# Starting TensorE's streamed operands and the split weights on 256-byte lines of SBUF

## The reference: what is computed

```python
# first block, two layers
h = h + rmsnorm(hgrn2_mixer(rmsnorm(h)))          # x @ w_in (1024 x 4096), gated recurrence, @ w_out
h = h + rmsnorm(conv_ffn(rmsnorm(h)))             # up (1024 x 2*2752), 3-tap conv, silu(gate)*value, down
h = h + rmsnorm(fox_mixer(rmsnorm(h), shared_kv)) # forget-gate attention, 16 heads
h = h + rmsnorm(conv_ffn(rmsnorm(h)))
# second block, two layers, each with shift, scale and gate from silu(c) @ ada_w + ada_b
x = x + gate * gdn_mixer(norm(x))                 # gated delta rule, 8 heads
x = x + gate * swiglu(norm(x))                    # gate and up (1024 x 2816 each), down
x = x + gate * mla_mixer(norm(x))                 # latent attention with rotary part
x = x + gate * swiglu(norm(x))
out = rmsnorm(x)
```

## The kernel before

| tensor | streamed width (columns) | row pitch in bytes | first row begins at (mod 256) | matmuls |
|---|---|---|---|---|
| `w_hi`, `w_lo` | stationary, 128 | 512 | 64 and 64 | all |
| `x_hi_a`, `x_lo_a` (HGRN in) | 272 | 1088 | 128 and 128 | 768 |
| `x_hi_b`, `x_lo_b` (HGRN out) | 272 | 1088 | 128 and 128 | 192 |
| `x_hi_up0`, `x_lo_up0` | 272 | 1088 | 128 and 128 | 1032 |
| `a_hi_up0`, `a_lo_up0` (down 0) | 272 | 1088 | 128 and 0 | 528 |
| `x_hi_c`, `x_lo_c` (Fox in) | 272 | 1088 | 128 and 128 | 600 |
| `fox_heads` (Fox out), from column 14 | 258 | 2176 | 184 | 192 |
| `x_hi_up1`, `x_lo_up1`, from column 14 | 258 | 1088 | 184 and 184 | 1032 |
| `a_hi_up1`, `a_lo_up1` (down 1) | 256 | 1024 | 128 and 128 | 528 |
| `x_hi_e`, `x_lo_e` (GDN in and out) | 256 | 1024 | 128 and 128 | 984 |
| `z_hi`, `z_lo` (gu0, gu1, MLA in) | 258 | 1032 | 128 and 192 | 2256 |
| `a_hi_gu`, `a_lo_gu` (dn0, dn1) | 256 | 1024 | 0 and 0 | 1055 |
| `xq_hi`, `xq_lo` | 256 | 1024 | 32 and 32 | 108 |
| `xkv_hi`, `xkv_lo` | 256 | 1024 | 0 and 0 | 48 streamed |
| `mla_o_hi`, `mla_o_lo` | 256 | 1024 | 0 and 0 | 192 |

## Time and profile before

### The profile page before, as it was taken

The page is one execution under the profiler, slowest core; times in us unless marked ns, Lnnn a source line. Parts: engine busy times, 40 slices in busy tenths (PEclk is TensorE's granted clock), DMA queues, the critical chain, the costliest instruction groups (busy, mean ns, idle before and its releaser), DMA issues. The chain is left out here.

```text
span 1529.3 us, 28962 instructions
## 1 busy us (share of the span) xinstructions
PE 1436.7 (94%) x11237; PEld 1380.1 (90%) x11237; DVE 1051.7 (69%) x1798; ACT 777.2 (51%) x1259; POOL 270.9 (18%) x360
## 2 busy tenths in 40 slices
PE   7998899999889998999979899989999999999997
PEld 7998789999888777999977799989999998899997
DVE  7773777877878726888777745357877657687653
ACT  6645554453476544454436555565343456544342
POOL 2001001220033400122001244002333100132210
PEclk9999989999999988999999999999999999999999
DMA  8533435559433203665953211136775635385451
GB/s 326 190 111 138 165 129 202 211 195 354 176 142 118 100 30 123 234 226 180 363 222 110 87 60 64 69 112 230 277 270 201 228 110 179 111 303 202 142 184 50
DMA packets 45700, 264.68 MB, mean 173 GB/s; under 512 B 8736, under 2 KB 10016, under 8 KB 20512
## 3 DMA queue, kind: packets, MB, share of 16 engines
q1 hardware_dynamic: 45600, 263.33, 47.6%
HBM read 262.26 MB, written 1.05 MB: 172 GB/s over the span
## 5 line engine op out<-in xcount | busy, mean ns | idle before, releaser
L257 DVE TENSOR_TENSOR w_lo<-raw,w_hi 128x2048 fp32r<-128x2048 f32 (+3 forms) x204 | 418.7, 2057 | 177.5 <-ACT w_hi L249 174.4
L249 ACT ACTIVATE w_hi<-raw 128x2048 fp32r<-128x2048 f32 (+3 forms) x221 | 380.1, 1725 | 83.0 <-PE bank L1233 43.4
L469 PE MATMUL bank<-z_hi,w_hi 128*128 128x258 f32 x704 | 199.9, 284 | 0.0
L471 PE MATMUL bank<-z_hi,w_lo 128*128 128x258 f32 x704 | 198.5, 282 | 0.0
L470 PE MATMUL bank<-z_lo,w_hi 128*128 128x258 f32 x704 | 198.2, 282 | 0.0
L470 PE MATMUL bank<-x_lo_up,w_hi 128*128 128x272 f32 (+1 forms) x656 | 188.1, 287 | 0.0
L469 PE MATMUL bank<-x_hi_up,w_hi 128*128 128x272 f32 (+1 forms) x656 | 187.2, 285 | 0.0
L471 PE MATMUL bank<-x_hi_up,w_lo 128*128 128x272 f32 (+1 forms) x656 | 186.6, 284 | 0.0
L470 PEld LDWEIGHTS bank<-z_lo,w_hi 128*128 128x128 f32 x704 | 133.4, 190 | 0.1
L471 PEld LDWEIGHTS bank<-z_hi,w_lo 128*128 128x128 f32 x704 | 133.0, 189 | 0.0
L469 PEld LDWEIGHTS bank<-z_hi,w_hi 128*128 128x128 f32 x704 | 132.8, 189 | 0.1
(11 more groups left out here) (516 smaller groups left out, 3924.2 us busy)
## 6 DMA issues: line engine op xcount, KB each, us to landing
raw<-w_gu SPq DMA_DIRECT2D x44, 1024.0 KB, 4.8
raw<-w_up SPq DMA_DIRECT2D x42, 1024.0 KB, 4.8
work<-w_ada SPq DMA_DIRECT2D x27, 1024.0 KB, 4.9
raw<-w_down SPq DMA_DIRECT2D x32, 704.0 KB, 5.4
raw<-w_dn SPq DMA_DIRECT2D x32, 704.0 KB, 4.1
mod_w_down<-w_ada SPq DMA_DIRECT2D x16, 1024.0 KB, 6.9
raw<-w_a_in SPq DMA_DIRECT2D x15, 1024.0 KB, 5.0
raw<-w_gdn_qkv SPq DMA_DIRECT2D x12, 1024.0 KB, 4.8
```

Source lines behind the costliest of these rows:

```text
L249: act.activation(w_hi[:, s, 0:blocks * P], raw[:, s, 0:blocks * P], ACT.Copy).then_inc(hi_split.sem, 1)
L257: dve.tensor_tensor(w_lo[:, s, 0:blocks * P], raw[:, s, 0:blocks * P], w_hi[:, s, 0:blocks * P].bitcast(F32), ALU.subtract).then_inc(lo_sp ...
L469: pe.matmul(o, w_hi[:, s, b], x_hi[:, xk, cols[0]:cols[1]], start=begin, stop=False)
L471: last = pe.matmul(o, w_lo[:, s, b], x_hi[:, xk, cols[0]:cols[1]], start=False, stop=end)
```

## The change

Every three-pass operand for which there is room gets rows whose pitch is rounded up to a multiple of 256 bytes and whose streamed part begins on one; `lead` shifts the row so that column 14 falls on the line where the stream begins there. `w_hi` and `w_lo` begin on a line. `x_c`, `a_up0` and `fox_heads` only get an aligned first row: the pitches of 1088 and 2176 bytes stay, so that their rows go on from one phase to the next, and `fox_heads` still streams from column 14. The remaining edits find the room: small tensors share `small_columns`, `gate_tok` shrinks from 128 to 104 columns (and the copy that fills it), and three scratch tensors of MLA move onto rooms that are free by then (`rope_other` onto `angles`, `angle_turns` and `probs_turned_mla` onto the constants' `levels`). No matmul, wait or DMA is added or removed.

```diff
+LINE = 256
-        def sbuf(c, name, shape, dt=F32):
-            return c.enter_context(nc.sbuf_tensor(name, shape, dt))
+        def sbuf(c, name, shape, dt=F32, align=32):
+            return c.enter_context(nc.sbuf_tensor(name, shape, dt, align_bytes=align))
+
+        def rows_on_lines(c, name, rows, width, lead=0):
+            pitch = -(-(lead + width) * 4 // LINE) * LINE // 4
+            return sbuf(c, name, [P, rows, pitch], F32R, LINE)[:, :, lead:lead + width]
-        w_hi = sbuf(ctx, "w_hi", [P, SLOTS, ITEM], F32R)
-        w_lo = sbuf(ctx, "w_lo", [P, SLOTS, ITEM], F32R)
+        w_hi = sbuf(ctx, "w_hi", [P, SLOTS, ITEM], F32R, LINE)
+        w_lo = sbuf(ctx, "w_lo", [P, SLOTS, ITEM], F32R, LINE)
+        small = sbuf(ctx, "small_columns", [P, 23])
-                x_hi, x_lo = sbuf(phase, "x_hi_a", [P, KD, T1], F32R), sbuf(phase, "x_lo_a", [P, KD, T1], F32R)
+                x_hi, x_lo = (rows_on_lines(phase, n, KD, T1) for n in ("x_hi_a", "x_lo_a"))
...
-                x_hi, x_lo = sbuf(phase, "x_hi_b", [P, KD, T1], F32R), sbuf(phase, "x_lo_b", [P, KD, T1], F32R)
+                x_hi, x_lo = (rows_on_lines(phase, n, KD, T1) for n in ("x_hi_b", "x_lo_b"))
...
-                a_hi = sbuf(phase, f"a_hi_{up}", [P, FF_TILES, width], F32R)
+                a_hi = sbuf(phase, f"a_hi_{up}", [P, FF_TILES, width], F32R, LINE)
-                    x_hi = sbuf(inner, f"x_hi_{up}", [P, KD, T1], F32R)
+                    x_hi = rows_on_lines(inner, f"x_hi_{up}", KD, T1, -cols[0] % (LINE // 4))
...
-                x_hi, x_lo = sbuf(inner, "x_hi_c", [P, KD, T1], F32R), sbuf(inner, "x_lo_c", [P, KD, T1], F32R)
+                x_hi, x_lo = (sbuf(inner, n, [P, KD, T1], F32R, LINE) for n in ("x_hi_c", "x_lo_c"))
...
-                        dve.tensor_copy(tok[:, :, :], bank[2][:, 0:2 * P].rearrange("p (x c) -> p x c",
-                                                                                   x=2)).then_inc(tok_made.sem, 1)
+                        turned_rows = bank[2][:, 0:2 * P].rearrange("p (x c) -> p x c", x=2)
+                        dve.tensor_copy(tok[:, :, :], turned_rows[:, :, 0:BR + H]).then_inc(tok_made.sem, 1)
...
-                xkv_hi, xkv_lo = (sbuf(scope, n, [P, 2, SEQ], F32R) for n in ("xkv_hi", "xkv_lo"))
-                other = sbuf(scope, "rope_other", [P, 2, SEQ])
+                xkv_hi, xkv_lo = (rows_on_lines(scope, n, 2, SEQ) for n in ("xkv_hi", "xkv_lo"))
+                other = angles
-                pt = sbuf(scope, "probs_turned_mla", [P, 2, 3 * C])
+                pt = con("levels", 0, 6 * C).rearrange("p (x c) -> p x c", x=2)
...
-            heads = sbuf(outer, "fox_heads", [P, KD, 2, T1], F32R)
+            heads = sbuf(outer, "fox_heads", [P, KD, 2, T1], F32R, LINE)
-            x_hi, x_lo = sbuf(scope, "x_hi_e", [P, KD, SEQ], F32R), sbuf(scope, "x_lo_e", [P, KD, SEQ], F32R)
+            x_hi, x_lo = (rows_on_lines(scope, n, KD, SEQ) for n in ("x_hi_e", "x_lo_e"))
-            z_hi, z_lo = (sbuf(scope, n, [P, KD, SEQ + 2], F32R) for n in ("z_hi", "z_lo"))
+            z_hi, z_lo = (rows_on_lines(scope, n, KD, SEQ + 2) for n in ("z_hi", "z_lo"))
-                a_hi, a_lo = (sbuf(phase, n, [P, FF_TILES, SEQ], F32R) for n in ("a_hi_gu0", "a_lo_gu0"))
+                a_hi, a_lo = (rows_on_lines(phase, n, FF_TILES, SEQ) for n in ("a_hi_gu0", "a_lo_gu0"))
...
-                    xq_hi, xq_lo = (sbuf(early, n, [P, 3, SEQ], F32R) for n in ("xq_hi", "xq_lo"))
-                o_hi, o_lo = (sbuf(phase, n, [P, KD, SEQ], F32R) for n in ("mla_o_hi", "mla_o_lo"))
+                    xq_hi, xq_lo = (rows_on_lines(early, n, 3, SEQ) for n in ("xq_hi", "xq_lo"))
+                o_hi, o_lo = (rows_on_lines(phase, n, KD, SEQ) for n in ("mla_o_hi", "mla_o_lo"))
```

More of the change, by code:

```diff
@@ L124, in fused_model @@
         std_room = sbuf(ctx, "std", [P, ROOT_COLS])
-        root_tok = sbuf(ctx, "root_tok", [P, ROOT_COLS // SQUARE])
         rstd, std = rstd_room[:, 0:T1], std_room[:, 0:T1]
@@ L129, in fused_model @@
         modf = mod[:, :, :, :].rearrange("p l s k -> p (l s k)")
-        mod_sum = sbuf(ctx, "mod_sum", [P, 2, 2])
         c_row = sbuf(ctx, "c_row", [P, D])
         raw = sbuf(ctx, "raw", [P, SLOTS, ITEM])
-        w_hi = sbuf(ctx, "w_hi", [P, SLOTS, ITEM], F32R)
-        w_lo = sbuf(ctx, "w_lo", [P, SLOTS, ITEM], F32R)
+        w_hi = sbuf(ctx, "w_hi", [P, SLOTS, ITEM], F32R, LINE)
+        w_lo = sbuf(ctx, "w_lo", [P, SLOTS, ITEM], F32R, LINE)
+        small = sbuf(ctx, "small_columns", [P, 23])
+        root_tok, mod_sum = small[:, 0:9], small[:, 9:13].rearrange("p (l t) -> p l t", l=2)
+        eps_col, conv_last, gate_coef, norm_eps = small[:, 13:14], small[:, 14:20], small[:, 20:22], small[:, 22:23]
         bank = [ctx.enter_context(nc.psum_tensor(f"bank{i}", [P, 512], F32)) for i in range(8)]
@@ L948, in passed @@
                     s_.passed(n_)
-        eps_col = sbuf(ctx, "eps_col", [P, 1])
-        conv_last = sbuf(ctx, "conv_last", [P, 6])
         params_in, consts_in, c_in = sig("params_in"), sig("consts_in"), sig("c_in")
@@ L1550, in ffn_layer @@
             with ExitStack() as phase:
-                a_hi = sbuf(phase, f"a_hi_{up}", [P, FF_TILES, width], F32R)
-                a_lo = sbuf(phase, f"a_lo_{up}", [P, FF_TILES, width], F32R)
+                a_hi = sbuf(phase, f"a_hi_{up}", [P, FF_TILES, width], F32R, LINE)
+                a_lo = sbuf(phase, f"a_lo_{up}", [P, FF_TILES, width], F32R, LINE)
                 with ExitStack() as inner:
-                    x_hi = sbuf(inner, f"x_hi_{up}", [P, KD, T1], F32R)
-                    x_lo = sbuf(inner, f"x_lo_{up}", [P, KD, T1], F32R)
+                    x_hi = rows_on_lines(inner, f"x_hi_{up}", KD, T1, -cols[0] % (LINE // 4))
+                    x_lo = rows_on_lines(inner, f"x_lo_{up}", KD, T1, -cols[0] % (LINE // 4))
                     entry = NormEntry(lambda k: h[:, k, cols[0]:cols[1]], KD, cols, gain, x_hi, x_lo, shift=shift,
@@ L2152, in __init__ @@
                 rows = sbuf(scope, "gate_rows", [P, SEQ])
-                tok = sbuf(scope, "gate_tok", [P, 2, P])
-                coef = sbuf(scope, "gate_coef", [P, 2])
+                G, B, R, BR = 0, 32, 64, 96
+                tok = sbuf(scope, "gate_tok", [P, 2, BR + H])
+                coef = gate_coef
                 one_col = con("reset_hgrn", 0, 47)
-                norm_eps = sbuf(scope, "head_norm_eps", [P, 1])
                 Lo = sbuf(scope, "coupling_level", [P, 2, 4, C])
@@ L2159, in __init__ @@
                 late_q = sbuf(scope, "late_queries", [P, H, C])
-                G, B, R, BR = 0, 32, 64, 96
                 grown, beta, lean = (tok[:, :, i:i + H] for i in (G, B, R))
@@ L3214, in fused_model @@
                     positions = sbuf(inner, "positions", [P, SEQ], mybir.dt.int32)
-                    turned = Angles(angles, sbuf(inner, "angle_turns", [P, 2, SEQ]), positions)
+                    turned = Angles(angles, con("levels", 0, 2 * SEQ).rearrange("p (x t) -> p x t", x=2), positions)
                     dn0 = streamed_down("dn0", a_hi, a_lo, res2, squares, mod_room(inner, "dn0"),
@@ L3227, in fused_model @@
                 run(gdn, gdn_out, gu0, dn0, mla_in, mla)
-            a_hi, a_lo = (sbuf(scope, n, [P, FF_TILES, SEQ], F32R) for n in ("a_hi_gu1", "a_lo_gu1"))
+            a_hi, a_lo = (rows_on_lines(scope, n, FF_TILES, SEQ) for n in ("a_hi_gu1", "a_lo_gu1"))
             res3 = Streamed("a", "mla_out", False, mod[:, 1, 2, :], squares, z_hi, z_lo, mod[:, 1, 4, :], mod[:, 1, 3, :])
```

## The result

The changed kernel takes 1540.64 us (median of 4 runs, 1537.96 to 1542.70), the kernel before 1530.55 us (4 runs, 1528.38 to 1531.77): a ratio of 1.0061, 95% interval 1.0045 to 1.0078. It is 0.6% slower. The forecast was 1504 us with the range 1490 to 1528, and 0.11 for slower: the sign is wrong.

What follows compares the result with a forecast made beforehand. The prediction took the count of matmuls times their start-to-start distance as the bound. Gains of 6.8 + 8.6 + 12.3 = 27.7 us, less 1.4 and 1.1, left 25.2 us: from 1529.6 to 1504.4 us, range 1490 to 1528.

Steps and rivals of the forecast that it cites:

- What bounds the kernel: Over most of the span, time is the number of matmuls times the start-to-start distance; TensorE's matmuls cover 94%.
- `w_hi`, `w_lo` from 64 to 0: Aligning the weight buffers, in all three-pass matmuls: taken as 0, with a possible gain of 16 us or a loss.
- excess per line: Each 256-byte line an operand row touches costs 1.7 ns per matmul; used to price gains at 258 and 272 columns.
- rival D: Weights and operand both at 0 collide; `a_gu` and `mla_o` fall back to 117.6 ns, costing 5.2 us: 1535 us; chance 0.09.
- Rival A: Width is the cost, not the start; only 256-wide streams gain, 5.4 us: 1524 us; chance 0.26.
- Rival B: Aligned streams have an excess of 6.7 ns at any width; gain 33.5 us: 1496 us; chance 0.20.
- Rival C: Streams stay in one of two states and the start isn't what decides; nothing moves: 1530 us; chance 0.13.
- The feed of down 1: In down 1, DMA would need 0.95 instead of 0.92; if that doesn't fit, the 2.2 us of `a_up1` go.
- The rule on 16-byte lines: By the skill's 16-byte cachelines only the 258-wide operands could gain; set aside for 117.6 against 113.4 ns in the trace.

Runs made afterwards that it cites:

- experiment 7: Changed kernel with the weights back at 64 and the 258-wide operands `z` and `x_up1` at 128: 1522.91 us, ratio 0.9939 to the kernel before.
- Experiment 1: Kernel before with the weight buffers moved from 64 to 0 and every operand left in place: 1540.13 us, ratio 1.0055 to the kernel before.
- experiment 2: Changed kernel with the weights back at 64, operands still aligned: 1530.71 us, ratio 0.9981 to the kernel before.
- Experiment 4: Streams alone, no model: weights and operand each at 0 to 224 in steps of 32, at three widths; 256 columns took 113.3 to 120.1 ns.
- experiment 5: Streams alone: hi and lo buffers placed separately, and 16 starts per pair; weights 64, operand 0 gave 113.3 ns from 6 starts, 117.8 from 10.
- experiment 11: Changed kernel, weights left at 0, 256-wide operands at 112, 258-wide at 16, 272-wide at 192: 1515.53 us, ratio 0.9898 to the kernel before.
- experiment 6: Streams alone, operand at 0, other widths and shorter weight loads: 111.3 to 113.3 ns from 192 to 240 columns.

## Why the prediction was wrong, point by point

*What bounds the kernel* held. The time is the number of matmuls times their distance; in every kernel here the span moved as the sum over the streams did, to within 2 us, but for that of experiment 7: there the distances give -9.5 us and the profiled span fell by 4.6, with 3 us more of waits. No wait of the earlier trace rows moved by more than 2 us.

*"`w_hi`, `w_lo` from 64 to 0": this is the step that gave the wrong sign.* I took 0, "as the distance follows the streamed operand and not the weights in the earlier trace rows". Both streams of the earlier trace rows have the weights at 64, so those rows couldn't say this: one of the two variables never changed in them. Experiment 1 changed it with every operand in place and lost 8.4 us (0.0055 x 1530.6). The miss of 36 us has two parts, though: by experiment 2 the weights' place makes 10 (1540.6 less 1530.7), and the other 26 are the gains priced by the excess per line (below), which did not come.

*The argument against rival D.* I held that equal places can't be slow, because the 272-wide rows pass through equality and are not above `z` in excess per column. Experiment 4 shows that equality is slow at 256 columns (120.0, the upper end of what is found there apart from single 120.1s) and middling at 272 (125.3 of 123.3 to 126.7). An observation at one width was carried to another.

*Rival D* was the right mechanism in the right place: `a_gu` and `mla_o`, 1247 matmuls, deciding "as soon as the aligned streams that are fast today show over 115 ns". Its size was off: I priced it at 117.6 ns, the slower level that the trace before showed, and the level was 120.0, which it didn't show. That is 8.2 us instead of 5.2; the other 3.6 us are `x_e`, `a_up1`, `x_up1` and `z` less the gain at 272 columns, all of which D held still. A chance of 0.09 for it was too small for an edit that moves one of two things read at once.

*The excess per line, 1.7 ns, behind all three gains,* failed as well, and it is the larger part of the miss: of its 27.7 us, 2.5 came by the stream means of experiment 2. With `x_e` it should have been 113.4 and was 119.6. With the weights left at 64 the same aligned operands show what it would have been worth: `a_up1` and `x_e` at 115.9 and 115.7 ns instead of 113.4, `z` and `x_up1` at 120.8 instead of 115.9, `a_gu` at 115.5 instead of 113.4; only the 272-wide gained a good part of their price, `x_up0` 2.7 of 4.3 ns. Experiment 2's ratio of 0.998 says that the operand part alone was worth about nothing. The number of 256-byte lines that a row touches is no quantity of this problem: 112 is not a multiple of 256, its rows touch 5 lines, and with the weights at 0 it is the best place for 256 columns. That the array "waits a little for its operands in every matmul" was an inference from the excess; no run shows what the excess is made of. (A slip without effect: the three-pass matmuls are 9,515 by the layout table, not some 9,400.)

*Rival A*, that the width is the cost, held for 272 columns in this sense: no pair of places brought them under 123.3 ns. *Rival B* fell with the lines.

*Rival C* saw the two levels in the earlier trace rows and was right that they exist, 113.3 and 117.8 ns. The forecast set it aside since "`a_gu` and `mla_o` are fast nearly throughout". With the weights at 64 and the operand at 0 they are fast from 6 of 16 starts (experiment 5), so that they were so in the profiled run before owed something to how their stages begin, which is an inference. But C's conclusion, that the start address doesn't matter, is wrong: the pair of addresses decides which levels there are.

*The feed of down 1* (DMA at 0.92 in the earlier trace rows, asked for 0.95) never was the limit: in experiment 11 it is at 0.95 over 40 us, and TensorE waits nowhere in them.

*The rule on 16-byte lines* (the Trainium skill, SBUF — State Buffer, Specifications) was set against a trace that seemed to know only 256. The runs say something between: multiples of 16 bytes are not alike, as (0, 112) at 113.3 and (0, 0) at 120.0 ns show. But operands at an odd multiple of 8 bytes are mostly at the slow end, about 120 ns at 24, 40, 56 and 168 with the weights at 0.

Another page would have spoken against D. The Trainium skill (TensorE: Matmul & The Clock Gate, Step-by-step: what each phase is for) says that weights and streamed operand have read ports of their own, so that loading the next weights takes nothing from the running matmul. This case doesn't agree: with the operand where it was, the weights' place makes 120.0 ns of 113.4 (experiment 1). What they share inside the chip no run here shows.

## What to carry to other kernels

Where matmuls run one behind the other at full clock and the weight load takes about as long as the stream (here 111.3 ns at the least, by the narrow streams of experiment 6, beside 113 to 120), the two start addresses are a pair: before one of them is moved, measure the whole pair, with the stream alone, from several starts, and at each width used. Take over the places as measured; here a difference of places carried with the weights on a multiple of 32 bytes, and 16 bytes past one it did not at 256 and 272 columns. And an argument that "the cost follows A and not B" needs rows in which B takes more than one value.

## What the runs showed of the hardware that was not expected

- The distance of 256-wide float32r matmuls with a 128-column weight load runs from 113.3 to 130.0 ns by start addresses alone, with nothing else on the core. One column per cycle would be 106.7; no stream alone on the core settled under 113.3.
- A stream can have two lasting levels (113.3 and 117.8 ns at weights 64, operand 0); which one depends on the matmul ahead of it. The kernels with the 256-wide streams at this pair have times 14 us apart; 2867 matmuls at one level or the other differ by 13 us, so the levels are large enough to do it, but only one execution of each has a trace. After its start a stream can need up to 13 matmuls to settle, so short runs are slower in the mean (`x_e` at 115.5 ns in experiment 11). Other pairs settled on one level from all starts tried: (0, 112), (64, 176), (0, 0), (192, 0). That is no proof of one level: (64, 128) did so from eight starts, and the earlier trace rows show it at 113.3 ns once.
- From 192 to 240 columns the distance stays at 111.3 to 113.3 ns, and 64 columns take 111.7, so a stream with 128-column weight loads has a floor just under the 256-wide distance.
- At the places of experiment 11 what was measured on an otherwise idle core carried into the full kernel to within 0.5 ns in the stretches without stalls, with DMA at 0.36 to 0.60 and VectorE 44 to 85% busy. The effect needs no traffic of other engines. Not every pair carried so well: (64, 128) at 258 columns is at 122.2 ns alone and 118.7 in the kernel, (80, 96) at 116.8 alone and 117.9 in `x_up1`.

What makes the 6.7 ns that remain, and why weights 16 bytes past a multiple of 32 behave differently, is not settled by these runs.
